# One hybrid decoder step: row shuffle, block compression and pool mixing, in two stages and in one

## What is computed

```python
def compress_blocks(rows, w_cmp, pos_cmp):      # BLOCK = 64 tokens
    blk = rows.reshape(n, l // BLOCK, BLOCK, 2, N_KV_HEADS, HEAD_DIM) + pos_cmp[:, :, None, :]
    return jnp.einsum('nbjshd,sjde->nbshe', blk, w_cmp)

def pool_mix(u, hist, first_pos, w_pool, pool_scale):   # windows 2, 4, 8, 16; 128 channels each
    ext = jnp.concatenate([hist, u], axis=1)
    ...                                         # running means of each window
    pooled = means - u
    return einsum('ntgc,gcd->ntgd', pooled, w_pool) * pool_scale
```

## Time and profile before

| | |
|---|---|
| median of 3 runs | 1989.32 us |
| the profiled execution's own time | 1988.15 us |
| its span, first to last instruction | 1986.4 us |
| PE, DVE, ACT, POOL busy | 89%, 33%, 30%, 33% of the span |
| shuffle and compression | 293.5 to 383.3 us |
| pool mixing | 383.3 to 415.5 us |

### The profile page before, as it was taken

The page is one execution under the profiler, slowest core; times in us unless marked ns, Lnnn a source line. Parts: engine busy times, 40 slices in busy tenths (PEclk is TensorE's granted clock), DMA queues, the critical chain, the costliest instruction groups (busy, mean ns, idle before and its releaser), DMA issues. The chain is left out here.

```text
span 1986.4 us, 26123 instructions
## 1 busy us (share of the span) xinstructions
PE 1773.0 (89%) x10956; PEld 1639.5 (83%) x10956; DVE 649.6 (33%) x1174; ACT 593.7 (30%) x1083; POOL 647.8 (33%) x451
## 2 busy tenths in 40 slices
PE   6899976668889888897699989899999999999997
PEld 2799965557777777775599989899999999999996
DVE  2411114243445554553144546310121121012135
ACT  3322211034445554553043435320121022002311
POOL 1454531024445553542013456222122112212421
PEclk9899996879999998998699999999999999999998
DMA  8343415301110100001264213211111111111411
GB/s 277 85 126 97 128 49 165 90 25 43 47 36 29 36 26 22 26 22 49 62 196 133 64 43 108 54 54 43 48 49 44 43 54 44 43 46 50 128 62 57
DMA packets 215048, 139.28 MB, mean 70 GB/s; under 512 B 53397, under 2 KB 211265, under 8 KB 214889
## 3 DMA queue, kind: packets, MB, share of 16 engines
q1 hardware_dynamic: 200171, 124.14, 21.8%
q10 hardware_dynamic: 14758, 13.44, 2.1%
HBM read 117.95 MB, written 21.92 MB: 70 GB/s over the span
## 5 line engine op out<-in xcount | busy, mean ns | idle before, releaser
L2032 POOL TENSOR_TENSOR ff_lo<-ff_raw,ff_hi 128x1024 fp32r<-128x1024 f32 x56 | 137.0, 2449 | 485.5 <-ACT ff_hi L1848 485.5
L1290 POOL TENSOR_SCALAR prob<-prob,share 128x16 f32<-128x16 f32 (+8 forms) x180 | 199.0, 1124 | 267.8 <-DVE share L1326 267.7
L1120 PE MATMUL gate_ps<-h_hi,gate_w_hi 128*128 128x344 f32 x384 | 142.9, 372 | 15.5 <-ACT gate_sum L1247 8.2
L2209 PE MATMUL ff_acc<-h_hi,ff_hi 128*128 128x344 f32 x672 | 142.6, 321 | 0.6 <-DVE relu_c L2358 0.6
L2209 PE MATMUL ff_acc<-h_lo,ff_hi 128*128 128x344 f32 x672 | 142.6, 320 | 0.0
L1336 DVE TENSOR_TENSOR p_lo<-pT,p_hi 128x512 fp32r<-128x512 f32 (+1 forms) x148 | 101.9, 688 | 122.6 <-ACT p_hi L1229 121.7
L2209 PE MATMUL ff_acc<-h_hi,ff_lo 128*128 128x344 f32 x672 | 141.9, 319 | 0.0
L1229 ACT ACTIVATE p_hi<-pT 128x512 fp32r<-128x512 f32 (+1 forms) x148 | 88.3, 597 | 164.8 <-PE pT L1174 164.3
L172 POOL TENSOR_TENSOR w_lo<-w_raw,w_hi 128x512 fp32r<-128x512 f32 (+1 forms) x31 | 56.3, 1820 | 233.1 <-ACT w_hi L168 143.8
L1218 ACT ACTIVATE prob<-scores,bias 128x640 f32<-128x640 f32 (+7 forms) x192 | 105.8, 557 | 78.8 <-DVE bias L1312 47.4
L1120 PE MATMUL gate_ps<-h_lo,gate_w_hi 128*128 128x344 f32 x384 | 127.0, 331 | 0.0
(11 more groups left out here) (375 smaller groups left out, 4059.2 us busy)
## 6 DMA issues: line engine op xcount, KB each, us to landing
ff_raw<-in_w_ff_dram SPq DMA_DIRECT2D x56, 512.0 KB, 3.8
wa_rest<-in_w_ada_dram SPq DMA_DIRECT2D x16, 1024.0 KB, 5.3
gate_spill<-gate_sum SPq DMA_DIRECT2D x48, 172.0 KB, 1.8
gates<-gate_spill SPq DMA_DIRECT2D x16, 516.0 KB, 5.5
wa<-in_w_ada_dram SPq DMA_DIRECT2D x8, 1024.0 KB, 9.8
gate_w_raw<-in_w_in_dram SPq DMA_DIRECT2D x16, 512.0 KB, 4.1
w_raw<-in_w_in_dram SPq DMA_DIRECT2D x30, 256.0 KB, 6.4
xt<-in_x_prompt_dram ACTq DMA_DIRECT2D x4, 1024.0 KB, 9.2
```

What stands on the lines that cost most here:

```text
L1120: last = pe.matmul(gps[:, 0:CH], a[:, u % 2, k], h[:, k, c * CH:(c + 1) * CH], start=(k == 0 and n == 0), stop=(k == KD - 1 and n == 2))
L1290: last = pool.tensor_scalar(y, y, share[:, n // 2 % 2, g, which:which + 1], None, ALU.mult)
L2032: pool.tensor_tensor(lo, raw, hi.bitcast(F32), ALU.subtract).then_inc(wflo_ready, 1)
L2209: last = pe.matmul(accs[s][:, c, 0:CH], w[:, z % SLOTS, k], x[:, k, c * CH:(c + 1) * CH], start=(k == 0 and n == 0), stop=(k == KD - 1 and ...
```

## The change

The two blocks become one, with one barrier less. What is done in them changes in these ways:

- **Pairs of tokens on the partitions.** `catT` becomes `pairsT`: the partition holds channel and parity of the token, and the two heads stand one after the other along the row. A compression matmul then sums over two tokens at once, and one 128x64 weight serves both heads. There are 64 matmuls of 97 columns against 64 (before 128 of 49 against 128), and the weights come once, in 8 transfers of 256 KB, into a ring of four that needs no zeros. The projection's copies write the pairs by stride-2 reads of PSUM, 8 copies for each of two products.
- **Pieces.** The compressed branch's token rows get pieces of their own (E_CT, 256 tokens, through `ctok`, output runs of 2 KB); the token pieces shrink to four transposes (L955). A page piece is copied in two halves: DVE takes head 0, ACT head 1 (`page_pairs`), each by two stride-2 copies, and `slot` waits for both. The small new-token pieces move to the front, the page table's load into the projection.
- **Pool sums in the same block.** After its last piece DVE runs the subtractions of the keys (L1030), then the window sums. PE places the four mixing products between the compression matmuls. Work on `crows` and `kcT` goes from DVE to ACT.
- **Places.** `pooled`, `hist` and `wp` lie over `kvT` and `gT`; the gate weights lie over the ring and the sums, so their first two loads wait for those, and ACT cuts them at its end.

```diff
--- before.py
+++ after.py
-        catT = at("catT", [P, 2, NCAT * BLOCK])
+        pairsT = at("pairsT", [P, 2, NROW * PAIR])
...
+                    sp.dma_start(pt_sb[:], page_table.rearrange("n (o g) -> o (n g)", o=1)).then_inc(page_loaded, 16)
...
-                            dve.tensor_copy(catT[:, k, 0:2 * CH].rearrange("p (c t) -> p c t", c=2), accs[s][:, 0:2, 0:CH])
-                            dve.tensor_copy(catT[:, k, 2 * CH:TP], accs[s][:, 2, 0:TP - 2 * CH])
+                            for kv in range(KVH):
+                                for j2 in range(2):
+                                    to = pairsT[rows_of(j2), k, kv * HEAD_AT:kv * HEAD_AT + TP // 2]
+                                    dve.tensor_copy(to[:, 0:CH].rearrange("p (c t) -> p c t", c=2),
+                                                    accs[s][rows_of(kv), 0:2, 0:CH].rearrange("p c (t j) -> p c t j", j=2)[:, :, :, j2])
+                                    dve.tensor_copy(to[:, CH:TP // 2],
+                                                    accs[s][rows_of(kv), 2, 0:TP - 2 * CH].rearrange("p (t j) -> p t j", j=2)[:, :, j2])
...
+            NWC = PAIR // JC
+            RWC = 4
-            NWC = BLOCK // JC
-            RWC = 2
-            wc = at("wc", [P, RWC, JC, P])
...
+            wc = at("wc", [P, RWC, JC, HD])
...
+            pooled = buf.slabs(2, kv_at)("pooled", [P, 4, T])
+            at = buf.slabs(2, g_at)
+            hist = at("hist", [NS * HIST, PW])
...
+                if q >= RWC:
                     eng.wait_ge(wc_used, q - RWC + 1)
                 s, c = divmod(q, NWC)
-                eng.dma_start(wc[h * HD:(h + 1) * HD, q % RWC, :, h * HD:(h + 1) * HD], w_cmp[0, s, c * JC:(c + 1) * JC].rearrange("j d e -> d j e"))\
+                eng.dma_start(wc[:, q % RWC], w_cmp[0, s, 2 * c * JC:2 * (c + 1) * JC].rearrange("(p j) d e -> (j d) p e", j=2))\
                    .then_inc(wc_loaded[q % RWC], 16)
...
+            def page_pairs(n, kv, j2):
+                c = kv * HEAD_AT + TP // 2 + n * P
+                src = tp[E_CK[n] % 2][rows_of(kv), 0:4 * P].rearrange("p (s t j) -> p s t j", s=2, j=2)
+                return pairsT[rows_of(j2), :, c:c + P], src[:, :, :, j2]
...
                     for q in range(RWC, 2 * NWC):
-                        load_wc(sp, 1, q)
+                        load_wc(sp, q)
...
+                    sp.wait_ge(wc_used, 2 * NWC)
+                    load_gate(sp, 0)
+                    sp.wait_ge(pooled_ready, 4)
+                    load_gate(sp, 1)
...
+                    def take_mix(g):
+                        act.wait_ge(mixed_done, g + 1)
+                        act.activation(by_chunk(uT[:, g]), pp[:, :, 0:CH], ACT.Copy, scale=vecs[:, V_POOL + g:V_POOL + g + 1])\
+                           .then_inc(mix_taken, 1)
...
+                    act.activation(gT[:], gT[:], ACT.Sigmoid).then_inc(gates_ready, 1)
                     for q in range(RWC):
-                        load_wc(act, 0, q)
-                    act.activation(gT[:], gT[:], ACT.Sigmoid).then_inc(gates_ready, 1)
+                        load_wc(act, q)
+                    act.wait_ge(tp_taken, E_NEW + 1)
...
                     for b in range(NB):
+                        if b % 2 == 0:
+                            x = b // 2
+                            act.wait_ge(tp_taken, E_CT[x] + 1)
+                            act.dma_start(n_cmp_p[0, 0, x * 2 * P:(x + 1) * 2 * P].rearrange("(t j) a h d -> t (j a h d)", j=2),
+                                          ctok[:, x % 2]).then_inc(ctok_out[x % 2], 16)
                         act.wait_ge(tp_taken, E_TOK[b] + 1)
...
+                        act.dma_start(n_sel_p[0, 0, b * P:(b + 1) * P].rearrange("t a h d -> t (a h d)"), t[:, 0:256]).then_inc(tok_out[b % 2], 16)
...
+                        act.wait_ge(tp_done, E_CK[b] + 1)
+                        for j2 in range(2):
+                            dst, src = page_pairs(b, 1, j2)
+                            last = act.activation(dst, src, ACT.Copy)
+                        last.then_inc(ck_taken, 1)
...
+                    take_mix(0)
+                    take_mix(1)
+                    act.wait_ge(wc_used, 2 * NWC)
+                    act.activation(crows[:], cps[:], ACT.Copy).then_inc(crows_ready, 1)
+                    take_mix(2)
...
+                    take_mix(3)
...
+                    for u in range(2):
+                        cut_gate_hi(act, u)
...
+                        if e - 2 in E_CK:
+                            pe.wait_ge(ck_taken, E_CK.index(e - 2) + 1)
...
+                    def compress(q):
+                        s, c = divmod(q, NWC)
+                        pe.wait_ge(wc_loaded[q % RWC], 16 * (q // RWC + 1))
+                        rows = pairsT[:, s].rearrange("p (b j) -> p j b", j=PAIR)
+                        for jj in range(JC):
+                            j = c * JC + jj
+                            last = pe.matmul(cps[:, s], rows[:, j], wc[:, q % RWC, jj], start=(j == 0), stop=(j == PAIR - 1))
+                        last.then_inc(wc_used, 1)
+                    def mix(g):
+                        if g == 0:
+                            pe.wait_ge(wp_loaded, 16)
+                        else:
+                            pe.wait_ge(mix_taken, g)
+                        pe.wait_ge(pooled_ready, g + 1)
+                        for c in range(NCH):
+                            last = pe.matmul(pp[:, c, 0:CH], wp[:, g], pooled[:, g, c * CH:(c + 1) * CH], start=True, stop=True)
+                        last.then_inc(mixed_done, 1)
...
-                    pe.wait_ge(tp_taken, E_VC)
-                    for q in range(2 * NWC):
-                        s, c = divmod(q, NWC)
-                        pe.wait_ge(wc_loaded[q % RWC], 32 * (q // RWC + 1))
-                        rows = catT[:, s].rearrange("p (b j) -> p j b", j=BLOCK)
-                        for jj in range(JC):
-                            j = c * JC + jj
-                            last = pe.matmul(cps[:, s], rows[:, j], wc[:, q % RWC, jj], start=(j == 0), stop=(j == BLOCK - 1))
...
+                    for b in range(NB):
...
+                    pe.wait_ge(tp_taken, E_HIST)
+                    pe.wait_ge(ck_taken, NS)
+                    for q in range(4):
+                        compress(q)
+                    mix(0)
+                    for q in range(4, 6):
+                        compress(q)
+                    mix(1)
+                    for q in range(6, 2 * NWC):
+                        compress(q)
+                    mix(2)
...
+                    mix(3)
...
+                            for j2 in range(2):
+                                last = dve.tensor_copy(*page_pairs(E_CK.index(e), 0, j2))
...
-                    dve.wait_ge(wc_used, 2 * NWC)
-                    dve.tensor_copy(crows[:], cps[:]).then_inc(crows_ready, 1)
...
+                    for i in range(2):
+                        dve.wait_ge(ctok_out[i], 16 * 2)
+                    dve.wait_ge(tp_done, E_HIST + 1)
+                    dve.tensor_copy(ext[:, :, :, 0:HIST], tp[E_HIST % 2][:, 0:4 * NS * HIST].rearrange("p (g n t) -> p g n t", g=4, n=NS))\
+                       .then_inc(tp_taken, 1)
+                    chain.then_wait(dve.tensor_copy(ext[:, :, :, HIST], uT[:, :, TP:T]))
...
+                        if g == 1:
+                            dve.wait_ge(vlo_ready, NB)
+                            for i in range(2):
+                                dve.wait_ge(tok_out[i], 16 * (4 + 2))
...
-                @block.tensor
-                def _(pe):
-                    pe.wait_ge(wp_loaded, 16)
-                    for g in range(4):
-                        pe.wait_ge(pooled_ready, g + 1)
-                        if g >= 2:
-                            pe.wait_ge(mix_taken, g - 1)
-                        for c in range(NCH):
-                            last = pe.matmul(pp[g % 2][:, c, 0:CH], wp[:, g], pooled[:, g, c * CH:(c + 1) * CH], start=True, stop=True)
-                        last.then_inc(mixed_done, 1)
```

More of the change, by code:

```diff
@@ new lines, in hybrid_step @@
+            crows = buf.small("crows", [NROW, 2, HD])
+            utok = buf.small("utok", [P, PW])
+            NEW_U, NEW_KV, NEW_WIN = 32, 64, 96
+            tp = [psum(st, f"sh_tp{i}", [P, 1024]) for i in range(2)]
+            cps = psum(st, "cps", [NROW, 2, HD])
+            pp = psum(st, "pp", [P, NCH, 512])
+            pos_loaded, ck_loaded = sem("pos_loaded"), [sem(f"ck_loaded{i}") for i in range(2)]
+            wc_loaded = [sem(f"wc_loaded{i}") for i in range(RWC)]
+            tp_done, tp_taken, ck_taken, wc_used = sem("tp_done"), sem("tp_taken"), sem("ck_taken"), sem("wc_used")
@@ new lines, in hybrid_step @@
+            hist_loaded, wp_loaded, pooled_ready, mixed_done, mix_taken, gd_loaded = (
+                sem(n) for n in ("hist_loaded", "wp_loaded", "pooled_ready", "mixed_done", "mix_taken", "gd_loaded"))
```

(34 more changed lines are left out.)

334 lines of the change are left out of this document (154 added, 180 removed).

## The result

The changed kernel takes 1940.1 us (median; 1938.95 to 1940.21, a disturbed run left out), the kernel before 1989.3: the ratio is 0.9751, 95% interval 0.9732 to 0.977. 1938 was forecast, 1930 to 1952 the range. In the profiled execution (span 1938.2 us) the new stage runs from 292.8 us to the attention's first memset at 366.3, 73.5 us, where the two stages of before took 122.0. What lies behind it takes 1571.9 us, and took 1570.9 (1986.4 less 415.5).

The account below looks back on a forecast made before the run. Two stages of 122.0 us, PE with its weights then DVE with its sums, were taken as chains that could run side by side. Ending at 364.1 instead of 415.5 saves 51.4 us: 1936.8, as median 1938 us, range 1930 to 1952.

Parts of the forecast that it names:

- Up to the first page piece: Stage start at 293.5 us: ACT's list of instructions and issues sums to 14.5 us, first page piece taken at 308.0.
- Seven more pieces: Page piece loop: a chain of PE, DVE and ACT at 2.6 us a piece, 18.2 us, last piece taken at 326.2.
- VectorE's row: DVE after the last piece: subtractions, history and short copy 5.6 us, window sums 20.2, together 25.8, ready at 352.0.
- PE's row: PE beside the sums: 128 compression records, three mixing products and the history's turn, 26.9 us, ending at 353.1.
- The end: Stage tail: last mixing product, ACT's emptying, gate cuts with POOL's two last, and the barrier, ending at 364.1 us.
- the mechanism's own range: Whole kernel: 1932 to 1947 us, from spreads in issues, pieces, products at half clock, and PE never being behind.
- the weight load bounds: Compression on PE: loading 97 columns sets each record at 0.245 to 0.41 us, PE 18 us later, 1956 us; chance 11%.
- The first rule weighed: Compression weight loads: 81 ns for 97 columns, 10.4 us for 128 loads, PE never late, result 2 us lower.
- Strided halves: Page piece loop: a stride-two half copy costs 0.84 us, adding 6.7 to 13.4 us, 1945 to 1951; chance 7%.
- The second rule: Page piece copies from PSUM: accesses leaving their 8-byte line each time pay, which spoke against the change.
- Late output buffers: Outputs on ACT's queue behind 1 MB of weights: `tok` held 8 us three times, 24 us, 1962 us; chance 3%.
- The gate products: Attention: interleaved high and low weight parts slow the gate products; at 15% the time is 2002 us; chance 2%.

Follow-up runs that it names:

- experiment 6: Changed kernel with the first gate-weight cast on ScalarE before the last mix is taken and the second subtraction moved from GpSimd to VectorE: 1938.1 us.
- swapped and side by side: Changed kernel with compression operands swapped (64 weight columns loaded, 97 columns of rows moving) and those 97 read side by side, not 32 elements apart: 1938.1 us.

## Why the prediction was right

The forecast of 1938 us was 2 us low, and the likeliest case is the one that came. Step by step, from the stage's start:

- *Up to the first page piece*: 308.0 forecast, 304.1 measured, 0.7 of it because the stage began earlier. The sum added ScalarE's issues to its instructions. They lie beside them:

```profile
292.79 1.28 ACT L825 ACT_TABLE_LOAD   x1 [10.12 <-PEq L568]
292.85 1.67 ACTq L766 DMA_DIRECT2D wc<-in_w_cmp_dram  x3
...
298.70 2.02 ACT L839 ACTIVATE k_st<-kvT 64x1032 fp32r<-64x1032 f32 x2 [3.55 <-DVE pairsT L1010]
299.87 0.37 ACTq L845 DMA_DIRECT2D out_dram<-ctok  x1
```

Three weight issues run beside the table load, another issue beside the key casts. The nearest rows had the size of an issue, not that it overlaps.
- *Seven more pieces*: 18.2 us forecast, 19.4 measured, 2.77 each. The chain of three engines held; what it lacked is the 6.3 us in which PE waits for cache pages.
- *VectorE's row*: 25.8 us forecast, 25.9 measured (323.48 to 349.37). The third window took 5.71 us; 5.74 was the price without POOL beside it, so that choice was right.
- *PE's row*: 26.9 us forecast, from 326.2; measured 32.3 (323.5 to 355.8). This is the step that was mis-sized, in two terms: the records 21.9 us instead of 18.5 (0.17 each at either clock, where 0.206 and 0.124 were taken), and three products 10.7 us instead of 7.3 (mostly half clock in place of 0.81). The turn of the history, 1.1 us in the sum, ran ahead of the row. PE was to be one microsecond behind VectorE, and is 6.4.
- *The end*: 11.0 us from the third product to the memset forecast, 10.5 measured, with POOL's cuts last; experiment 6 shows that they set the end.
- *Sum*: -3.9 + 1.2 + 5.4 - 0.5 = 2.2 us, from 364.1 to 366.3. The mechanism held, but that the figure is this close is partly luck: two errors of 4 and 5 us had opposite signs. The lower end of the mechanism's own range was added up too low, too: 1938 less 1.3, 1.4 and 2 is 1933, not 1932.

Where the 49 us of the stage come from cannot be added up from the experiments, since they share PE's row, but each has its price there: 128 more records 21.1 us (the old ones were only 14.9 dearer than the new), the overlap 14.1, the ring of four 6.4. What the barrier that fell away was worth was not tested.

The rivals: *the weight load bounds* had the right place and the wrong price. A load of 97 columns does set the record, but at 0.17 us, not at 0.245 and 0.41; the middle between the bounds was nearer. The first rule weighed, the Trainium skill, "TensorE: Matmul & The Clock Gate", section "LDWEIGHTS (loading the stationary operand)", gives a load's time as its columns over 1.2, in ns; an estimate from it is 81 ns for 97 columns. The runs show 90 at the upper clock for columns side by side, so there it nearly agrees, and 168 at the lower clock or with the stride, where it does not. *Strided halves* is refuted: 417 and 378 ns, and in the piece loop PE waits 6.3 us for pages, 1.3 for half copies. The second rule, the Trainium skill, "SBUF — State Buffer", section "Door 1: The DMA port swizzle (why `[64,N]` ≈ `[32,N]`)", spoke of accesses that leave their line each time; the copies from PSUM with a stride of two do not bear it out, but TensorE's strided columns from SBUF agree with it at the upper clock (168 against 90 ns a record); at the lower they cost no more than columns side by side (168 to 170). The rule was weighed at the wrong place. *Late output buffers*: the waits show none. *The gate products*: 

```profile
L1178 PE MATMUL gate_ps<-h_hi,gate_w_cut 128*128 128x344 f32 x768 | 232.5, 351 | 15.5 <-ACT gate_sum L1305 8.2 <-POOL gate_w_cut L713 6.8
...
L1178 PE MATMUL gate_ps<-h_lo,gate_w_cut 128*128 128x344 f32 x384 | 126.9, 330 | 0.0
```

The two groups that share the high parts are one line now, 768 records of 351 ns, and the third has 384 of 330. Before, the two groups had 372 and 330 ns, 351 on average:

```profile
L1120 PE MATMUL gate_ps<-h_hi,gate_w_lo 128*128 128x344 f32 x384 | 126.8, 330 | 0.0
```

The part behind the stage is 1.0 us longer than before, so this rival is refuted.

## What to carry to other kernels

When two chains are laid side by side, price both rows to the end at both clock levels: the gain is at most the shorter one (here 14.1 us, with sums of 20.2 beside records of 21.9), and what was hidden under the longer (here the gate cuts) becomes the tail. Price a matmul with few moving columns by the columns that it loads as well, and look whether they lie side by side; a trial that reads the same tile in another order costs one line. Before a load is blamed for its size, deepen its ring: the wait went although the landing grew. It comes back when the row before it gets faster: PE waits 4.0 us for the same ring of four in the kernel that is swapped and side by side.

## What the hardware showed that was not expected

- TensorE's time for 97 fp32 columns is 0.16 to 0.17 us a record when they lie 32 elements (128 bytes) apart, at clock 0.50 and 1.00 alike, loaded or moved; side by side it is 0.168 to 0.170 at 0.50 and 0.090 to 0.093 at 1.00.
- Two executions of one kernel were granted different clocks in the same place: a mixing product took 3.75 us in one and 1.95 in the other, 3.5 us over the four. Filling the gaps ahead with work did not hold the clock up: it fell from 1.00 to 0.50 with PE busy throughout.
- ScalarE issues transfers beside its own instructions: three issues, 1.67 us, beside a table load of 1.28.
- An issue can take long: of four weight loads on SyncE one issue took 5.6 us, the others 0.4 to 0.8:

```profile
L766 SPq DMA_DIRECT2D wc<-in_w_cmp_dram x4: 367/582/5608, 326.6 to 337.6; - x4
```
